# A 1-layer hybrid encoder step: expert rows picked by a 0/1 matrix on TensorE instead of indirect gathers

## What is computed

```python
g_logits = (xt @ w_group) + b_group                  # 4 groups
g_idx = argmax(g_logits); g_w = softmax(g_logits)[g_idx]
e_sel = (einsum('nd,dge->nge', xt, w_router) + b_router)[rows, g_idx]   # 4 experts of the group
top_v, top_i = top_k(e_sel, 2); top_w = softmax(top_v) * g_w
combine = sum(one_hot(g_idx*4 + top_i, 16) * top_w)  # two experts of 16 per token
for e in range(16):                                   # xt (320, 1024), expert width 512
    h = silu(xt @ w_gate[e]) * (xt @ w_up[e])
    y = y + combine[:, e:e+1] * (h @ w_down[e])
z = layer_norm(2**0.25 * z + y)
```

## Time and profile before

| | us |
|---|---|
| median of 3 runs | 638.3 |
| lowest, highest | 636.44, 639.0 |
| the profiled execution, its device time | 637.03 |
| its span, first to last instruction | 635.2 |

### The profile page before, as it was taken

How to read it: one execution, slowest core, us unless ns; L and a number is a source line. 1 busy time by engine, 2 the same in 40 slices (tenths; PEclk the granted TensorE clock), 3 DMA queues, 4 the chain that set the end, 5 groups by cost and what they waited for, 6 DMA issues and landing times.

```text
span 635.2 us, 9071 instructions
## 1 busy us (share of the span) xinstructions
PE 536.4 (84%) x3552; PEld 393.7 (62%) x3553; DVE 230.0 (36%) x488; ACT 133.5 (21%) x245; POOL 68.5 (11%) x87
## 2 busy tenths in 40 slices
PE   4789989999999999999973699899787898687840
PEld 1789956887889798878663465555443455354410
DVE  2925985777332223113346021211111111111177
ACT  3344287852512122100020000000000000000010
POOL 4160730000000000010000710100000000000210
PEclk9999989877999999999975799999879799989895
DMA  8237791402156879790075389999999999999642
GB/s 220 98 97 219 191 297 44 134 1 68 33 194 203 299 247 313 268 358 10 33 308 205 100 318 385 381 387 376 391 397 401 414 412 410 397 423 426 252 124 83
DMA packets 55213, 157.49 MB, mean 248 GB/s; under 512 B 3558, under 2 KB 36034, under 8 KB 51076
## 3 DMA queue, kind: packets, MB, share of 16 engines
q1 hardware_dynamic: 46464, 135.11, 57.0%
q0 software_dynamic: 4896, 13.92, 7.6%
q10 hardware_dynamic: 3812, 7.88, 3.5%
HBM read 145.10 MB, written 11.78 MB: 247 GB/s over the span
## 4 chain that ended last, share of the span: by engine, by line
PE 66%; DMA 15%; DVE 7%; issue 4%; ACT 3%; SPq 3%; DVEq 0%; POOL 0%; POOLq 0%; ACTq 0%
PE bank L1031 20%; DMA expert_slots<-in_w_up 10%; PE bank L842 8%; PE bank L992 7%; PE bank L829 6%; PE bank L830 6%; PE bank L831 6%; SPq L590 3%; PE bank L917 3%; PE bank L1024 2%; DMA z_rows<-work 2%; PE bank L811 1%; PE bank L897 1%; PE bank L812 1%; PE bank L813 1%
## 5 line engine op out<-in xcount | busy, mean ns | idle before, releaser
L1031 PE MATMUL bank<-expert_slots,work 128*64 128x256 f32 (+3 forms) x1584 | 190.2, 414 | 30.8 <-DMA expert_slots<-in_w_gate 12.3
L1031 PEld LDWEIGHTS bank<-expert_slots,work 128*64 128x64 f32 (+1 forms) x1584 | 105.3, 138 | 104.3 <-issue 48.9
L829 PE MATMUL bank<-z_high,weights_high 128*128 128x320 f32 (+1 forms) x256 | 81.8, 319 | 0.4 <-DVE weights_low L536 0.4
L830 PE MATMUL bank<-z_low,weights_high 128*128 128x320 f32 (+1 forms) x256 | 80.2, 313 | 0.0
L831 PE MATMUL bank<-z_high,weights_low 128*128 128x320 f32 (+1 forms) x256 | 80.0, 313 | 0.0
L1749 DVE SCALAR_TENSOR_TENSOR work<-work,bank 128x256 f32<-128x256 f32 (+1 forms) x18 | 7.3, 406 | 142.4 <-ACT work L1316 136.5
L842 PE MATMUL bank<-work,expert_slots 128*128 128x320 f32 x192 | 52.3, 432 | 0.0
L536 DVE TENSOR_TENSOR weights_low<-expert_slots,weights_high 128x2048 fp32r<-128x2048 f32 x19 | 43.5, 2288 | 22.8 <-ACT weights_high L531 22.7
L829 PEld LDWEIGHTS bank<-z_high,weights_high 128*128 128x128 f32 x256 | 49.1, 192 | 1.6 <-DVE weights_low L536 0.7
L830 PEld LDWEIGHTS bank<-z_low,weights_high 128*128 128x128 f32 x256 | 48.9, 191 | 0.2
L831 PEld LDWEIGHTS bank<-z_high,weights_low 128*128 128x128 f32 x256 | 48.7, 190 | 0.0
(11 more groups left out here) (252 smaller groups left out, 566.1 us busy)
## 6 DMA issues: line engine op xcount, KB each, us to landing
expert_slots<-in_w_gate SPq DMA_DIRECT2D x16, 2048.0 KB, 28.9
expert_slots<-in_w_up SPq DMA_DIRECT2D x16, 2048.0 KB, 31.6
expert_slots<-in_w_down SPq DMA_DIRECT2D x15, 2048.0 KB, 28.7
expert_slots<-in_w_in SPq DMA_DIRECT2D x19, 1024.0 KB, 5.8
expert_slots<-in_w_branch_rnn SPq DMA_DIRECT2D x4, 1024.0 KB, 7.2
expert_slots<-in_w_out SPq DMA_DIRECT2D x4, 1024.0 KB, 5.8
expert_rows<-work ACTq DMA_DIRECT2D x30, 128.0 KB, 8.4
expert_rows<-work POOLq DMA_DIRECT2D x6, 384.0 KB, 10.6
```

The lines of the kernel that those rows point to most:

```text
L829: nc.tensor.matmul(b[:, 0:NALL - lo], wh[:, k, o], zh[:, k, lo:NALL], start=(k == 0), stop=False)
L830: nc.tensor.matmul(b[:, 0:NALL - lo], wh[:, k, o], zl[k // 4][:, k % 4, lo:NALL], start=False, stop=False)
L1031: mm = nc.tensor.matmul(bank[m * j:m * j + m, cols], lhsT(k), rhs(k, j), start=(k == 0), stop=(k == kk - 1))
```

## The change

Rows are no longer gathered from DRAM for the 16 items. DVE makes for each item a 0/1 matrix `pick` [tokens, 96 slots] from the ranks (`pick_item`, one instruction of 128x288). PE multiplies it with `rows` (`choose`: 3 token tiles times 2 halves of the width, 6 matmuls with 64 stationary columns and 512 moving), which gives the first 64 rows of the item in one bank, half the width on partitions 0 to 63 and half on 64 to 127. ACT copies the bank (`take_rows`), PE transposes it (`turn_chosen`, 4 transposes instead of 8), DVE copies two blocks of 128x256 to `xT`. The second 32 rows are picked behind the branch (`choose_rest`: 12 matmuls with 32 stationary columns, 2 transposes; `rest_columns`: 3 copies on DVE). Indirect gathers stay for overflow items alone, and the write of `z1_rows` with them.

The ranks take 3 matmuls instead of 9, with DVE adding up the one-hot matrices first (`e_upto`). The list of token numbers is made by the same 6 matmuls, moved behind item 0 (`overflow_index`). The scaling of `rows` moves from POOL to ACT, to item 15. The DVE loop over the items is written out. Only the last part of `e_sum` is masked. Buffers move within `work`.

The diff, cut to the parts that are spoken of:

```diff
-        xg = [ea.take(D) for _ in range(3)]
+        pick = [ea.take(3, CAP) for _ in range(3)]
+        xg = ea.take(D)
+        rows_of = ea.take(512)
+        rest_of = ea.take(256)
         xT = [ea.take(KD, CAP) for _ in range(3)]
-        yo = [ea.take(512) for _ in range(3)]
         th_a, hid_a, hT_a = ea.take(256), ea.take(256), ea.take(256)
         th_b, hid_b, hT_b, yo_b = ea.take(P), ea.take(P), ea.take(P), ea.take(256)
-
-
...
-            def scale_residual():
-
-                for j in range(3):
-                    for h in range(2):
-                        S.emptied(pool, ("z1T", j, h))
-                for j in range(3):
-                    n = OUT_ROWS[j]
-                    nc.gpsimd.tensor_scalar(rows[0:n, j, :], rows[0:n, j, :], ALPHA, None, ALU.mult).then_inc(rows_scaled2, 1)
-
-            def gather(i, s):
+            def gather(i):
                 nc.gpsimd.indirect_dma_start(
-                    out=xg[s][0:CAP, :], out_offset=None, in_=z1_dram[:, :],
-                    in_offset=bass.IndirectOffsetOnAxis(ap=index_i[0:CAP, i:i + 1], axis=0)).then_inc(xg_in[s], 16)
-
+                    out=xg[0:CAP, :], out_offset=None, in_=z1_dram[:, :],
+                    in_offset=bass.IndirectOffsetOnAxis(ap=index_i[0:CAP, i:i + 1], axis=0)).then_inc(xg_in, 16)
 
             pool.wait_ge(route_done, 1)
             pool.wait_ge(z1_out, 48)
-            for i in range(NE):
-                if i >= 3:
-                    pool.wait_ge(xt_full, i - 2)
-                gather(i, i % 3)
-                if i == 2:
-                    scale_residual()
...
+            flat = "p j e -> p (j e)"
+            nc.tensor.matmul(b[:, 0:NE], before, e_sum[:, 0, :], start=True, stop=True)
+            nc.tensor.matmul(b[:, NE:4 * NE], ones, e_upto.rearrange(flat), start=True, stop=False)
+            nc.tensor.matmul(b[:, NE:3 * NE], before, e_sum[:, 1:3, :].rearrange(flat), start=False, stop=True)\
+                .then_inc(S.f_full("ranks"), 1)
+
+            def overflow_index():
+
+                pe.wait_ge(selected, 1)
+                for k in range(2):
+                    for j in range(3):
+                        mm = nc.tensor.matmul(YB[0:CAP, 0:NITEM], rank_hot[:, k, CAP * j:CAP * j + CAP],
+                                              item_hot[:, k, NITEM * j:NITEM * j + NITEM],
+                                              start=(k == 0 and j == 0), stop=(k == 1 and j == 2))
+                mm.then_inc(index_full, 1)
+
+            def picked(bank, cols, s, at, n):
+
+                parts = P // n
                 for j in range(3):
-                    mm = nc.tensor.matmul(b[0:CAP, 0:NITEM], rank_hot[:, k, CAP * j:CAP * j + CAP], item_hot[:, k, NITEM * j:NITEM * j + NITEM],
-                                          start=(k == 0 and j == 0), stop=(k == 1 and j == 2))
-            mm.then_inc(S.f_full("index"), 1)
-            pe.wait_ge(route_done, 1)
-
-
-            def turn(i, s, n):
-
-                pe.wait_ge(xg_in[s], 16 * (n + 1))
+                    m = OUT_ROWS[j]
+                    z = rows[0:m, j, :].rearrange("t (p k) -> t p k", k=KD)
+                    for q in range(parts):
+                        mm = nc.tensor.matmul(bank[n * q:n * q + n, cols], pick[s][0:m, j, at:at + n],
+                                              z[:, :, KD // parts * q:KD // parts * (q + 1)], start=(j == 0), stop=(j == 2))
+                return mm
+
+            def choose(i, s):
+
+                pe.wait_ge(pick_made, i + 1)
+                picked(TB[0], slice(0, 512), s, 0, FIRST).then_inc(pick_full, 1)
+
+            def turn_chosen(i):
+
+                pe.wait_ge(pick_taken, i + 1)
                 wait_past(pe, xt_made, i)
-                cols = xg[s][0:CAP, :].rearrange("c (p k) -> c k p", k=KD)
+                four = rows_of.rearrange("c (p k) -> c k p", k=4)
+                for k in range(4):
+                    mm = nc.tensor.transpose(TB[1][:, P * k:P * k + P], four[:, k, :], ident)
+                mm.then_inc(xt_full, 1)
+
+            def choose_rest(s, b):
+
+                picked(BB, slice(0, 256), s, FIRST, REST).then_inc(rp_full, 1)
+                pe.wait_ge(rp_taken, b + 1)
+                two = rest_of.rearrange("c (p k) -> c k p", k=2)
+                for k in range(2):
+                    mm = nc.tensor.transpose(BB[:, 256 + P * k:256 + P * k + P], two[:, k, :], ident)
+                mm.then_inc(xr_full, 1)
+                pe.wait_ge(xr_made, b + 1)
+
...
-            pe.wait_ge(ctrl_done, 1)
 
             def round_of(n, first):
                 for s in range(3):
                     i = 3 * n + s
+                    choose(i + 1, (s + 1) % 3)
                     hidden(i, s, n, ha_full)
+                    if first and s == 1:
+                        pe.wait_ge(route_done, 1)
                     if not (first and s == 0):
                         down(i - 1, (s - 1) % 3, n if s else n - 1)
-                    turn(i + 1, (s + 1) % 3, n + (s + 1) // 3)
+                    turn_chosen(i + 1)
+                    if first and s == 0:
+                        pe.wait_ge(ctrl_done, 1)
                     maybe_rest(i, s, n)
                     turn_hidden(ha_made, i + 1, hta_full)
-
-            turn(0, 0, 0)
+                    if first and s == 0:
+                        overflow_index()
+
+            choose(0, 0)
+            turn_chosen(0)
...
+            def take_rows(i):
+
+                act.wait_ge(pick_full, i + 1)
+                nc.scalar.copy(rows_of, TB[0][:, :]).then_inc(pick_taken, 1)
+
+            take_rows(0)
 
             def round_of(n, first):
                 for s in range(3):
                     i = 3 * n + s
+                    take_rows(i + 1)
                     gate_tanh(s, ha_full, i + 1, ha_tanh)
                     if not (first and s == 0):
                         rows_out(i - 1, (s - 1) % 3, n if s else n - 1, i - 1)
+                    if first and s == 0:
+                        act.wait_ge(ctrl_done, 1)
                     maybe_rest(i)
 
...
+            for j in range(3):
+                n = OUT_ROWS[j]
+                nc.scalar.mul(rows[0:n, j, :], rows[0:n, j, :], ALPHA).then_inc(rows_scaled2, 1)
...
-            tt(e_sum, e_sum, bc(cst("valid").unsqueeze(2), 3, NE), ALU.mult).then_inc(chosen, 1)
+            step(tt(e_sum[:, 2, :], e_sum[:, 2, :], cst("valid")[:, 2:3].to_broadcast([P, NE]), ALU.mult))
+            step(tt(e_upto[:, 1, :], e_sum[:, 0, :], e_sum[:, 1, :], ALU.add))
+            step(V.tensor_copy(e_upto[:, 0, :], e_sum[:, 0, :]))
+            step.settle()
+            tt(e_upto[:, 2, :], e_upto[:, 1, :], e_sum[:, 2, :], ALU.add).then_inc(chosen, 1)
...
+            def pick_item(i):
+
+                slot = cst("iota_cap").unsqueeze(1).to_broadcast([P, 3, CAP])
+                mine = pick_rank[:, :, i].unsqueeze(2).to_broadcast([P, 3, CAP])
+                stt(pick[i % 3], slot, 1.0, mine, ALU.add, ALU.is_equal).then_inc(pick_made, 1)
+
+            def columns(i, s):
+                dve.wait_ge(xt_full, i + 1)
+                turned = TB[1][:, :].rearrange("p (k j c) -> p k j c", j=2, c=FIRST)
+                for j in range(2):
+                    cp = V.tensor_copy(xT[s][:, 4 * j:4 * j + 4, 0:FIRST], turned[:, :, j, :])
+                cp.then_inc(xt_made, 1)
+
             b = S.arrived(dve, "ranks")
+            alone(stt(pick_rank, b[:, 0:3 * NE].rearrange("p (j e) -> p j e", e=NE), 1.0, e_sum, ALU.add, ALU.mult))
+            for i in range(3):
+                pick_item(i)
...
             step.settle()
+            columns(0, 0)
             alone(stt(base, ov_end, float(NE - 1), ov, ALU.add, ALU.subtract))
...
+            def rest_columns(s, b):
+                dve.wait_ge(rp_full, b + 1)
+                V.tensor_copy(rest_of, BB[:, 0:256]).then_inc(rp_taken, 1)
+                dve.wait_ge(xr_full, b + 1)
+                turned = BB[:, 256:512].rearrange("p (k j c) -> p k j c", j=4, c=REST)
+                dst = xT[s].rearrange("p (j k) c -> p k j c", k=2)[:, :, :, FIRST:CAP]
+                for k in range(2):
+                    cp = V.tensor_copy(dst[:, k], turned[:, k])
+                cp.then_inc(xr_made, 1)
 
...
+            for i in range(LAST):
+                silu_first(i + 1, i % 3)
+                columns(i + 1, (i + 1) % 3)
+                maybe_rest(i)
+                hidden_columns(i + 1)
+                if i == 0:
+                    dve.wait_ge(index_full, 1)
+                    V.tensor_copy(index_i[0:CAP, :], YB[0:CAP, 0:NITEM]).then_inc(route_done, 1)
+                if i + 3 < NE:
+                    pick_item(i + 3)
```

67 lines of the change are left out of this document (31 added, 36 removed).

## The result

The changed kernel takes **677.85 us** (median of 4 runs, 677.14 to 679.05), the kernel before 638.65 (4 runs, 636.44 to 640.18): a ratio of 1.065, 95% interval 1.061 to 1.070. The prediction, 633 with a range of 626 to 644, was wrong in size and in sign. Medians are of all executions; a ratio and its interval leave out those that took over 1.5% longer than the fastest of the same kernel.

A forecast was written before the change was run, and what follows sets the result against it. PE and DMA engines were nearly even; after the change PE alone sets the end. -7.3 to expert 14's up product, +4.2 unpriced, -0.6 and -0.9 in the tail make -4.6: 633 us predicted, range 626 to 644.

The forecast's parts named there:

- The start: Before expert 0: its products start at 347.5 instead of 356.06, 8.5 us earlier; bounds 346.5 and 351.
- rival D: Start of the expert stage: both choices at half clock, start 351 instead of 347.5, total 636.5 us; chance 0.10.
- One choose: Picking matmuls on PE: 3 pairs of 512 columns at 0.88 each, 2.64 us per choose at full clock.
- One expert: PE's period per expert: 10.56 + 0.53 + 0.37 + 2.64 = 14.1 us instead of 12.7.
- what no row prices: Per expert on PE: sequencer loads and branches plus choose's strided operand and 64-row tile, 0.3 us together, +4.2 over 14 experts.
- The second 32 rows: Experts 1 and 10: extra time rises from 7.3 by 3.6 to 10.9 us each.
- The weights: Expert 14's up matrix lands at 552, needed at 573, so weights are early and PE alone sets the end.
- The tail: Behind expert 14: -0.6 from shorter transposes and copy, -0.9 from the last down product's clock; ACT's scaling of rows zero.
- Term (a): PE's sequencer loads two words and branches between row and hidden transposes, less hidden by 4 transposes: 0 to 0.6 us per expert.
- a sign of being wrong: Idle time on "issue" ahead of the hidden transposes above 0.6 us would show the prediction wrong.
- Rival A: Picking dearer than its columns, by stride or tiling modes; at half speed 2.64 more per choose, +42, 675 us; chance 0.20.

The follow-up runs named there:

- run with one branch: Changed kernel, PE's loop keeping the branch for the second 32 rows in only one of three places: 642.1 us, ratio 1.002 to the kernel before.
- a fraction of the weights: Changed kernel and kernel before, each loading for items 3 to 14 only one of eight gate/up and one of four down slices: 667.5 and 606.4 us.

## Why the prediction was wrong, step by step

- **The start** was forecast at 347.5 (bounds 346.5 to 351), 8.5 us earlier than before; it is at 345.69, of which 8.0 us are the change's; it lies under the lower bound only by the 2.4 us ahead of the change. Right. From the first rank matmul to the first product it is 11.4 us in place of 19.3. Where both pickings ran at half clock, as in the profiled run with one branch (5.58 and 5.22), it is 14.8: rival D was real in some executions.
- **One choose** at 2.64: 2.87 to 2.88 from its start to the next product (355.61 to 358.49). The unpriced 0.24 is the strided operand and the change of tiles together; which of them, no run shows.
- **One expert** at 14.1, and 14.4 with the 0.3 for what no row prices: 14.26. Right.
- **The second 32 rows** at 10.9: 383.66 - 358.49 - 14.26 = 10.9. Right, by rows that had to be put together from five places.
- **The weights** early, and PE alone at the end: right. No wait for an expert's weights is left; a gate matrix lands 12.9 us after its issue in place of 28.9.
- **The tail**: forecast 60.7 us from item 14's first product to the end of the span (630.6 - 569.9), measured 61.7 (675.5 - 613.85). The number is right by luck. It has a wait of 4.60 on "issue" ahead of item 15's hidden transposes that wasn't forecast, and item 14's down product takes 5.35 as before, where I had taken off 0.9. Against it, DVE's next step comes 1.9 us behind the start of PE's last products (654.21 to 656.14) in place of 5.6 (610.27 to 615.87): in the kernel before it was still adding gathered rows, and I had no term for that.
- **Term (a), "PE's sequencer loads two words and branches", 0 to 0.6 us per expert**, is the step that failed. Item 14 started at 613.85, not at 569.9 (565.7 + 4.2). The 43.9 us are 33.7 of "issue" up to there (21.4 at three jumps back, 11.7 at jumps forward, 0.5 inside products) and 12.4 of half clock, nearly all behind the jumps back, less 1.8 for the earlier start and 2.4 by which undisturbed items came out below the forecast; 2.0 more were lost around these waits, mostly 0.2 beside each one ahead of the hidden transposes. I had read the one row with 0.50 on "issue" as a cost of a branch, and had priced branches at 0 to 0.6; the jumps forward were 0.6 to 3.3 and the jumps back 6.9 to 7.7. That row lies in the first pass of the loop, where the kernel before still fetches, and what it should have made me ask is how much code lies between a jump and its target, and whether the body still stays with the engine. The prediction did name this wait as a sign of being wrong, but with another cause.
- **Rival A** gave 675 us and the kernel took 677.9. Its mechanism is false: the picking cost 0.24 more than its columns, not 2.64. A time that fits is not a cause.

No view of the profile before shows code length as a cost, because in that kernel it was none. Two numbers were there, though: 30 packets of instructions, with none from 460 to 580 us, and the text of the loop, which grew from 393 to 441 matmuls. What one can't get from them is the edge, which only a run with padding shows.

## To carry to other kernels

When a change lengthens the body of a loop, count the instructions of each engine in it, never-run branches included, and look at the instruction queue by windows: the loops here that were kept had fetches in their first pass only. If it is near the edge, the cheapest experiment is one with never-run code added. And where two resources are nearly even, work that is put on the one that waits is free only up to its slack; here it was 30 us, and the picking used them.

## What the hardware showed

- A loop of PE with 393 or 405 float32 matmuls and transposes in its body (1506 and 1554 instructions in the profile's way of counting, 4 for a matmul and 2 for a transpose) runs its later passes without a fetch. With 441 or 489 (1698 to 1710, and 1890) 8 to 11 packets are fetched per 60 us, and each jump back stalls PE for 6.9 to 7.8 us. The Trainium skill, "Runtime: NRT & Kernel Launch", section Instruction fetch mechanics, says that code is fetched in order in blocks of 16 KiB, into 128 KiB on this engine, and that a taken branch to a target outside what is held stalls for a fetch. The packets of 16.4 KB and both kinds of stall agree with it. An edge at 1554 to 1698 instructions, waits and branches not counted, lies below the 2048 that the page gives for this size. The window of two blocks that the page gives for a branch doesn't fit a loop of 1506 instructions that runs without a fetch.
- With a fraction of the weights these stalls are still 5.4 to 6.0 us. In the one looked at the DMA engines are 0.85 to 0.94 busy for over half of it, so that is not shown to be the price of a fetch by itself.
- A forward jump over 374 never-run instructions costs 0.6 to 3.3 us in the changed kernel's loop, and 4.0 once in the run with one branch; with a fraction of the weights 0.6 to 1.2. Over 450 (two branches in a row, with 32 never-run matmuls) it is up to 5.0.
- Each long stall is paid twice. The granted clock is 1.00 before it and 0.50 in it and behind it, and the next picking and, behind two of the three, a part of the next products ran at half speed, 2.4 to 4.6 us for each stall of 7.
- The written-out loop needs no jump back and still fetches its code behind full queues: it gave 16 of 39 us back in the changed kernel and lost 0.5% in the old one.
